# The delta rule's doubling levels with the upper chunk one bank behind the lower, and six remainders placed later in VectorE's order

## The chip, the cores and the metric

The program runs on one core of a Trainium2 chip. The metric is the device time of one execution in microseconds (us); before the change it is 2875.41 us, the median of three runs (2873.04 to 2876.01).

## The reference, cut to what matters

A 512-token sequence of width 1024 passes two layers of a first block and one layer of a second block. All matrices are float32. In each layer of the first block a quarter of the mixing width is a recurrent mixer of 4 heads of 64:

```python
def step(S, inp):
    r_t, w_t, k_t, v_t, kk_t, a_t = inp
    s_kk = jnp.einsum('bhvk,bhk->bhv', S, kk_t)
    S = (S * w_t[:, :, None, :] - s_kk[..., None] * (kk_t * a_t)[:, :, None, :]
         + v_t[..., None] * k_t[:, :, None, :])
    return S, jnp.einsum('bhvk,bhk->bhv', S, r_t)
...
mixed = jnp.concatenate([y_att, y_rwkv, y_conv], axis=-1) @ w_mix_out[l]
```

The second block has a gated delta rule of 8 heads, which the reference itself cuts into chunks of 64 tokens and solves with the inverse of a lower triangular matrix:

```python
a = jnp.einsum('bhnid,bhnjd->bhnij', k_beta, kc) * decay_strict
t_inv = lax.linalg.triangular_solve(eye + a, jnp.broadcast_to(eye, a.shape),
                                    left_side=True, lower=True, unit_diagonal=True)
...
def step(state, inp):
    q_e, at, u_c, w_c, k_d, dec = inp
    v_new = u_c - jnp.einsum('bhck,bhkv->bhcv', w_c, state)
    o = jnp.einsum('bhck,bhkv->bhcv', q_e, state) + jnp.einsum('bhij,bhjv->bhiv', at, v_new)
    state = state * dec[..., None, None] + jnp.einsum('bhck,bhcv->bhkv', k_d, v_new)
    return state, o
```

## The kernel before, in words

Most of the time is dense products of 128 by 128 weights with 512 tokens. The change touches only the recurrent mixers, which the kernel handles in chunks of 64 tokens, in both blocks by the same helpers, with a `Unit` object that names the tiles (`d_...` for the first block, once in each of its two layers; `gd_...` for the second block).

A group is 16 matrices of 64 by 64: four banks of PSUM (`level_bank(q)`, q = 0 to 3), in each two pairs j, and for each pair a lower chunk c = 0 on partitions 0 to 63 and an upper chunk c = 1 on partitions 64 to 127. The first block's mixer has 2 groups in each layer (4 chunks each), the second block's has 4 groups (2 chunks each): 8 groups in all. Each triangular inverse is built in five levels (LEVELS = 5, m = 0 to 4; 40 levels in all). A level is:

- `level_v_pe` on TensorE: for each bank q one product for each j and c (16 products). It waits for the masked factor `bt` from GpSimd (`delta_pool`) and, where m > 0, for the bank's subtraction of the level before (`delta_xy_ready`); in level 0 for `delta_start`, which VectorE gives for two banks at a time. After a bank it gives `delta_v1_summed`.
- `level_act` on ScalarE: copies the bank to `v1` and gives `delta_v1_ready`.
- `level_x_pe` on TensorE: for each bank the products for x (not in level 4) and y, for each j and c (32 products, 16 in level 4). After a bank it gives `delta_xy_summed`.
- `level_dve` on VectorE: subtracts the bank's sums from x and y (one instruction for each bank) and gives `delta_xy_ready`.

A product of chunk c reads 64 partitions and writes 64 partitions of the same half, so lower products lie in one 64 by 64 tile of TensorE's array and upper ones in the diagonally opposite tile. Each float32 product leaves two MATMUL records in the trace.

The inverse feeds a recursion over chunks: `read_pe` (L2143, L2151), `rhs_dve` (L2200, L2203), `solve_pe` (L2163, L2169), `u_act` (L2218), `update_pe` (L2179 to L2189), `state_dve` (L2210). The first group's levels run alone. In the first block (`rw_delta_pe`) the four chunks of the first group are then woven between the products of the second group's levels by a hand-written order; in that order a piece of the recursion stands between each x product and the next v product. In the second block (`gd_delta_pe`) the two chunks of group s are woven between the levels of group s + 1; there levels 0 and 1 follow each other directly. The last group's recursion runs alone. Every engine takes its instructions in the order in which they are written.

Six `others_low` instructions in each layer of the first block (L2295, on VectorE) form the low parts `hn_lo` of the six tiles of the mixed activations that the recurrent mixer doesn't make (four of attention, two of the convolution). TensorE wants them (`others_lo`) only after the whole recursion, for the output projection. Before the change four stand after levels 0 to 3 of the first group, and two among the second group's levels.

Of the kernel before, what the change touches and what calls it, by code (L numbers as in the profile page):

```python
# [12 lines left out]
P = 128  # L13
# [78 lines left out]
HD = 64  # L92
# [5 lines left out]
LEVELS = 5  # L98
# [23 lines left out]
OTHERS = (0, 1, 2, 3, 6, 7)  # L122


def program(nc, w, out):
# [23 lines left out]
    with ExitStack() as ctx:  # L149
# [262 lines left out]
        delta_bt_ready = sem("delta_bt_ready")  # L412
# [115 lines left out]
        def half(c):  # L528
            return slice(HD * c, HD * c + HD)

        def level_bank(q):
            return LEVEL_BANK + q
# [1510 lines left out]
        def level_v_pe(pe, d, s, m):  # L2043

            G = d.group + s
            i = LEVELS * G + m
            for q in range(4):
                pe.wait_ge(delta_bt_ready, 2 * i + q // 2 + 1)
                if m:
                    pe.wait_ge(delta_xy_ready, 4 * (i - 1) + q + 1)  # L2050
                else:
                    pe.wait_ge(delta_start, 2 * G + q // 2 + 1)
                for j in range(2):
                    for c in range(2):
                        last = pe.matmul(ps[half(c), level_bank(q), j * HD:(j + 1) * HD], d.bt[half(c), m % 2, q, j],  # L2055
                                         d.xy[half(c), q, j, 0], start=True, stop=True)
                last.then_inc(delta_v1_summed, 1)

        def level_x_pe(pe, d, s, m):

            i = LEVELS * (d.group + s) + m
            for q in range(4):
                pe.wait_ge(delta_v1_ready, 4 * i + q + 1)
                for j in range(2):
                    at = P + j * P
                    if m < LEVELS - 1:
                        for c in range(2):
                            pe.matmul(ps[half(c), level_bank(q), at:at + HD], d.xy[half(c), q, j, 1], d.v1[half(c), q, j],  # L2068
                                      start=True, stop=True)
                    for c in range(2):  # L2070
                        last = pe.matmul(ps[half(c), level_bank(q), at + HD:at + 2 * HD], d.v1[half(c), q, j], d.xy[half(c), q, j, 1],  # L2071
                                         start=True, stop=True)
                last.then_inc(delta_xy_summed, 1)

        def level_act(act, d, s, m):
            i = LEVELS * (d.group + s) + m
# [220 lines left out]
        def rw_delta_dve(dve, own, d, l):  # L2297
            rw_masks_dve(dve, d, 0)
            for m in range(LEVELS):
                if m == 0:  # L2300
                    rw_mc1_dve(dve, d, 0)
                level_dve(dve, d, 0, m)
                if m < LEVELS - 1:
                    others_low(dve, l, OTHERS[m])
            rhs_dve(dve, own, d, 0, 0)
            rw_masks_dve(dve, d, 1)
            state_dve(dve, d, 0, 0)
            rw_mc1_dve(dve, d, 1)
            rhs_dve(dve, own, d, 0, 1)
            level_dve(dve, d, 1, 0)  # L2310
            state_dve(dve, d, 0, 1)
            others_low(dve, l, OTHERS[4])
            level_dve(dve, d, 1, 1)
            rhs_dve(dve, own, d, 0, 2)
            others_low(dve, l, OTHERS[5])
            level_dve(dve, d, 1, 2)
            state_dve(dve, d, 0, 2)
            rhs_dve(dve, own, d, 0, 3)
            level_dve(dve, d, 1, 3)
            state_dve(dve, d, 0, 3)  # L2320
            level_dve(dve, d, 1, 4)
            for i in range(4):
                rhs_dve(dve, own, d, 1, i)
                state_dve(dve, d, 1, i)

        def spread_pe(pe, s):
# [597 lines left out]
```

## Time and profile before

| What | us |
|---|---|
| median of three runs | 2875.41 |
| the profiled execution | 2876.07 |
| its span in the profile | 2874.3 |
| TensorE busy | 2748.0 |
| VectorE busy | 1494.7 |
| ScalarE busy | 967.8 |
| GpSimd busy | 189.0 |

The three delta stages lie at 571 to 634 us, 1595 to 1659 us and 2561 to 2680 us of the span. Busy time is a union of the records of an engine. "PE" is TensorE's products, "PEld" its weight loads, "DVE" is VectorE, "ACT" ScalarE and "POOL" GpSimd. A stretch in which TensorE is busy need not be one in which it is at its peak: several tiles of its array can run at once, and a stretch in which only one runs counts the same.

### The profile page before, as it was taken

What the parts mean: (1) busy time and instruction counts of PE and PEld (TensorE: products, weight loads), DVE (VectorE), ACT (ScalarE), POOL (GpSimd) and SP (SyncE); (2) the same over time, 40 slices, a digit from 0 to 9 for tenths busy, and PEclk for the clock granted to TensorE, in tenths of its full rate; (3) what the DMA queues carried; (4) which work ended last, traced back from release to release, by engine and by line L of the source; (5) the groups of instructions that cost most, each with busy time, mean ns of one, the idle gap of its engine ahead of it and who ended that gap; (6) DMA issues with size and microseconds to landing.
All of it is one profiled execution on the core that took longest, in us unless ns stands there. A gap on an engine that the chain in (4) does not pass through costs nothing.

```text
span 2874.3 us, 42222 instructions
## 1 busy us (share of the span) xinstructions
PE 2748.0 (96%) x17756; PEld 2240.7 (78%) x17756; DVE 1494.7 (52%) x1845; ACT 967.8 (34%) x1471; POOL 189.0 (7%) x267
## 2 busy tenths in 40 slices
PE   6999999999999999999999899999999999968998
PEld 5888877687888878888777878888877777658787
DVE  6565565756565443333457644333365546755534
ACT  3222334523222332222345333222324444323322
POOL 3000000320000000000002300000010000013000
PEclk9999999989999999999999989999999999969999
DMA  7565542103566222232222012232232222100132
GB/s 287 200 218 203 191 167 72 52 18 112 202 207 220 88 85 102 86 112 88 95 80 71 3 59 90 88 108 93 90 103 74 66 74 69 61 1 3 56 103 73
DMA packets 46521, 299.68 MB, mean 104 GB/s; under 512 B 5664, under 2 KB 5792, under 8 KB 18080
## 3 DMA queue, kind: packets, MB, share of 16 engines
q1 hardware_dynamic: 37152, 230.35, 23.5%
q0 software_dynamic: 9216, 67.11, 6.5%
q8 instruction: 118, 1.93, 0.3%
q14 instruction: 35, 0.29, 0.0%
HBM read 295.35 MB, written 2.10 MB: 103 GB/s over the span
## 4 chain that ended last, share of the span: by engine, by line
PE 92%; DVE 5%; ACT 1%; DMA 1%; issue 1%; POOL 0%; SPq 0%; DVEq 0%; ACTq 0%
PE ps L921 18%; PE ps L922 18%; PE ps L923 18%; PE ps L1209 6%; PE ps L1210 6%; PE ps L1211 6%; PE ps L1516 2%; PE ps L1517 2%; PE ps L1518 2%; PE ps L2071 1%; PE ps L2055 1%; PE ps L2068 1%; DMA ada_first<-in_ada 1%; PE ps L1331 1%; PE ps L1295 1%
## 5 line engine op out<-in xcount | busy, mean ns | idle before, releaser
L921 PE MATMUL ps<-hn_hi,w_hi 128*128 128x512 f32 x1440 | 564.5, 392 | 16.9 <-DVE hn_lo L870 16.7
L922 PE MATMUL ps<-hn_lo,w_hi 128*128 128x512 f32 x1440 | 563.4, 391 | 0.0
L923 PE MATMUL ps<-hn_hi,w_lo 128*128 128x512 f32 x1440 | 562.9, 391 | 0.0
L897 DVE TENSOR_TENSOR w_lo<-w_raw,w_hi 128x2048 fp32r<-128x2048 f32 (+2 forms) x227 | 467.8, 2061 | 162.8 <-ACT w_hi L890 162.8
L890 ACT ACTIVATE w_hi<-w_raw 128x2048 fp32r<-128x2048 f32 (+2 forms) x227 | 390.6, 1721 | 100.0 <-PE ps L1211 97.3
L1209 PE MATMUL ps<-hn_hi,w_hi 128*128 128x512 f32 x776 | 323.6, 417 | 7.7 <-DVE hn_lo L870 4.9
L921 PEld LDWEIGHTS ps<-hn_hi,w_hi 128*128 128x128 f32 x1440 | 272.3, 189 | 75.3 <-issue 18.6
L923 PEld LDWEIGHTS ps<-hn_hi,w_lo 128*128 128x128 f32 x1440 | 272.3, 189 | 57.4
L922 PEld LDWEIGHTS ps<-hn_lo,w_hi 128*128 128x128 f32 x1440 | 272.4, 189 | 56.3
L1210 PE MATMUL ps<-hn_lo,w_hi 128*128 128x512 f32 x776 | 306.4, 395 | 0.0
L1211 PE MATMUL ps<-hn_hi,w_lo 128*128 128x512 f32 x776 | 305.8, 394 | 0.0
L921 PE MATMUL ps<-act_hi,w_hi 128*128 128x512 f32 x704 | 273.9, 389 | 0.0
L922 PE MATMUL ps<-act_lo,w_hi 128*128 128x512 f32 x704 | 273.9, 389 | 0.0
L923 PE MATMUL ps<-act_hi,w_lo 128*128 128x512 f32 x704 | 273.9, 389 | 0.0
L989 ACT ACTIVATE silu<-ps 128x512 f32<-128x512 f32 x88 | 52.7, 599 | 599.1 <-PE ps L923 599.1
L1035 DVE TENSOR_TENSOR act_f<-silu,ps 128x512 f32<-128x512 f32 x88 | 60.5, 687 | 370.5 <-ACT silu L989 370.5
L1209 PEld LDWEIGHTS ps<-hn_hi,w_hi 128*128 128x128 f32 x776 | 147.7, 190 | 54.4 <-issue 23.5
L1210 PEld LDWEIGHTS ps<-hn_lo,w_hi 128*128 128x128 f32 x776 | 148.3, 191 | 35.0 <-issue 6.2
L1211 PEld LDWEIGHTS ps<-hn_hi,w_lo 128*128 128x128 f32 x776 | 148.1, 191 | 32.5
L772 DVE CUSTOM_DVE_ANT_0 ada_w<-ada_w,c_row,b_ada 128x1024 f32<-128x1024 f32 x128 | 159.0, 1279 | 0.1
L1061 DVE SCALAR_TENSOR_TENSOR h<-act_f,out_gain,h 128x512 f32<-128x512 f32 (+1 forms) x64 | 48.1, 752 | 204.2 <-ACT act_f L1005 204.2
L923 PEld LDWEIGHTS ps<-act_hi,w_lo 128*128 128x128 f32 x704 | 132.1, 188 | 27.6
(470 smaller groups left out, 3630.9 us busy)
## 6 DMA issues: line engine op xcount, KB each, us to landing
w_raw<-in_up SPq DMA_DIRECT2D x88, 1024.0 KB, 4.9
ada_w<-in_ada POOLq DMA_DIRECT2D x64, 1024.0 KB, 5.2
w_raw<-in_down SPq DMA_DIRECT2D x64, 704.0 KB, 4.1
w_raw<-in_mix_in SPq DMA_DIRECT2D x20, 1024.0 KB, 4.9
w_raw<-in_dsa_in SPq DMA_DIRECT2D x18, 1024.0 KB, 4.9
w_raw<-in_merge SPq DMA_DIRECT2D x16, 768.0 KB, 4.3
ada_first<-in_ada SPq DMA_DIRECT2D x8, 1024.0 KB, 12.4
w_raw<-in_mix_out SPq DMA_DIRECT2D x8, 1024.0 KB, 4.9
```

The costliest lines, as they stand in the source:

```text
L772: last = dve.tensor_tensor_reduce(ws[:, t], ws[:, t], c_row[:], 1.0, b_ada[:, col:col + 1], ALU.mult, ALU.add, mod[:, col:col + 1])
L890: act.activation(w_hi[:, slot, 0:size], w_raw[:, slot, 0:size], ACT.Copy).then_inc(w_hi_ready, 1)
L897: dve.tensor_tensor(w_lo[:, slot, 0:size], w_raw[:, slot, 0:size], w_hi[:, slot, 0:size].bitcast(F32), ALU.subtract).then_inc(w_lo_ready, 1)
L921: pe.matmul(bank, wh, x_hi[:, k], start=(k == 0), stop=False)
L922: pe.matmul(bank, wh, x_lo[:, k], start=False, stop=False)
L923: return pe.matmul(bank, wl, x_hi[:, k], start=False, stop=(k == K - 1))
L1035: dve.tensor_tensor(act_f[:, s], silu[:, s], main[s][1], ALU.mult).then_inc(act_f_ready, 1)
L1209: pe.matmul(ps[:, t], wh, hn_hi[:, k], start=(k == 0), stop=False)
L1210: pe.matmul(ps[:, t], wh, hn_lo[:, k], start=False, stop=False)
L1211: last = pe.matmul(ps[:, t], wl, hn_hi[:, k], start=False, stop=(k == KD - 1))
L1516: pe.matmul(main[slot][t], wh, x_hi[:, kk], start=(kk == 0), stop=False)
L1517: pe.matmul(main[slot][t], wh, x_lo[:, kk], start=False, stop=False)
```

## The change

The products of a level keep their number, operands and results; their order and the places of the waits and signals change. Stage q of `level_v_pe` and of `level_x_pe` now holds the lower chunk's products of bank q beside the upper chunk's of bank q - 1, so there are five stages for four banks: in the first only lower products, in the last only upper ones. The wait for bank q stands ahead of the whole stage, and the signal for bank q - 1 after it. On VectorE the six `others_low` leave their places among the levels and stand in the last recursion of each layer, two each between `rhs_dve` and `state_dve` of the second group's chunks 0, 1 and 2 (`OTHERS` is (0, 1, 2, 3, 6, 7)).

```diff
+            def product(q, j, c):
+                return pe.matmul(ps[half(c), level_bank(q), j * HD:(j + 1) * HD], d.bt[half(c), m % 2, q, j],
+                                 d.xy[half(c), q, j, 0], start=True, stop=True)
+            for q in range(5):
+                if q < 4:
+                    pe.wait_ge(delta_bt_ready, 2 * i + q // 2 + 1)
+                    if m:
+                        pe.wait_ge(delta_xy_ready, 4 * (i - 1) + q + 1)
+                    else:
+                        pe.wait_ge(delta_start, 2 * G + q // 2 + 1)
                 for j in range(2):
-                    for c in range(2):
-                        last = pe.matmul(ps[half(c), level_bank(q), j * HD:(j + 1) * HD], d.bt[half(c), m % 2, q, j],
-                                         d.xy[half(c), q, j, 0], start=True, stop=True)
-                last.then_inc(delta_v1_summed, 1)
+                    if q < 4:
+                        product(q, j, 0)
+                    if q:
+                        last = product(q - 1, j, 1)
+                if q:
+                    last.then_inc(delta_v1_summed, 1)
...
+            for q in range(5):
+                if q < 4:
+                    pe.wait_ge(delta_v1_ready, 4 * i + q + 1)
                 for j in range(2):
                     if m < LEVELS - 1:
+                        if q < 4:
+                            x_product(q, j, 0)
+                        if q:
+                            x_product(q - 1, j, 1)
+                    if q < 4:
+                        y_product(q, j, 0)
+                    if q:
+                        last = y_product(q - 1, j, 1)
+                if q:
+                    last.then_inc(delta_xy_summed, 1)
...
                 level_dve(dve, d, 0, m)
-                if m < LEVELS - 1:
-                    others_low(dve, l, OTHERS[m])
...
             state_dve(dve, d, 0, 1)
-            others_low(dve, l, OTHERS[4])
             level_dve(dve, d, 1, 1)
             rhs_dve(dve, own, d, 0, 2)
-            others_low(dve, l, OTHERS[5])
...
             for i in range(4):
                 rhs_dve(dve, own, d, 1, i)
+                for j in OTHERS[2 * i:2 * i + 2]:
+                    others_low(dve, l, j)
                 state_dve(dve, d, 1, i)
```

## Rows read from the trace of the kernel before

**Rows 1.** The page: the chain that ended last, shares of the span by engine.

```profile
PE 92%; DVE 5%; ACT 1%; DMA 1%; issue 1%; POOL 0%; SPq 0%; DVEq 0%; ACTq 0%
```

**Rows 2.** Stretches: from:to, length, then busy us of each engine, granted clock.

```profile
core 0: us, PE busy (x) PEld busy (x) DVE busy (x) ACT busy (x) POOL busy (x), PEclk, DMA share, GB/s
594.00:620.00 26.00, 24.11 (x820) 23.74 (x812) 17.45 (x40) 7.81 (x27) 8.23 (x10) 1.00 0.02 4
...
2591.40:2594.80 3.40, 3.40 (x74) 3.40 (x70) 0.84 (x2) 0.55 (x2) 1.34 (x2) 0.50 0.02 5
...
625.40:639.00 13.60, 12.84 (x130) 9.66 (x125) 2.74 (x8) 4.81 (x7) 0.00 (x0) 0.50 0.00 1
```

**Rows 3.** TensorE in order of time, x products of level 2, both tiles at work.

```profile
586.92 0.31 PE L2068 MATMUL ps<-d_v,d_xy 64*64 64x64 f32 x4
587.04 0.31 PE L2071 MATMUL ps<-d_xy,d_v 64*64 64x64 f32 x4
587.16 0.31 PE L2068 MATMUL ps<-d_v,d_xy 64*64 64x64 f32 x4
```

**Rows 4.** TensorE around a solve, whose eight L2163 records share one tile.

```profile
616.50 0.45 PE L2163 MATMUL ps<-d_rhs,d_yf 64*64 64x64 f32 x5
616.74 0.27 PE L2169 MATMUL ps<-rw_vt,rw_kt 64*64 64x64 f32 x1
616.79 0.22 PE L2163 MATMUL ps<-d_rhs,d_yf 64*64 64x64 f32 x1
...
616.85 0.22 PE L2163 MATMUL ps<-d_rhs,d_yf 64*64 64x64 f32 x1
...
616.90 0.22 PE L2163 MATMUL ps<-d_rhs,d_yf 64*64 64x64 f32 x1
```

**Rows 5.** The same around a solve of the second block (16 records, one tile).

```profile
2604.80 0.27 PE L2055 MATMUL ps<-gd_xy,gd_bt 64*64 64x64 f32 x1
2604.85 0.22 PE L2163 MATMUL ps<-gd_rhs,gd_yf 64*64 64x64 f32 x1
...
2604.97 0.22 PE L2163 MATMUL ps<-gd_rhs,gd_yf 64*64 64x64 f32 x1
```

**Rows 6.** VectorE in order of time, levels 2 and 3 of a first group.

```profile
586.69 1.82 DVE L2089 TENSOR_TENSOR d_xy<-d_xy,ps 128x256 f32<-128x256 f32 x4 [0.50 <-PE ps L2071]
588.43 0.69 DVE L2295 TENSOR_TENSOR hn_lo<-proj,hn_hi 128x512 fp32r<-128x512 f32 x1
589.61 1.82 DVE L2089 TENSOR_TENSOR d_xy<-d_xy,ps 128x256 f32<-128x256 f32 x4 [0.50 <-PE ps L2071]
```

**Rows 7.** TensorE in order of time, the last bank's v products, the next x.

```profile
588.66 0.45 PE L2055 MATMUL ps<-d_xy,d_bt 64*64 64x64 f32 x8
588.91 0.22 PE L2068 MATMUL ps<-d_v,d_xy 64*64 64x64 f32 x1
```

**Rows 8.** TensorE's first v product of a group, and who TensorE waited for.

```profile
576.72 0.51 PE L2055 MATMUL ps<-d_xy,d_bt 64*64 64x64 f32 x10 [1.38 <-POOL d_bt L555]
...
PE ps L2055 <- DVE gd_xy L2369: 18.2, 8, 6.3
```

**Rows 9.** All six remainders of both layers: duration min/median/max in ns.

```profile
L2295 DVE TENSOR_TENSOR hn_lo<-proj,hn_hi x8: 683/684/686, 581.7 to 1615.3; 128x512 fp32r<-128x512 f32 x8
L2295 DVE TENSOR_TENSOR hn_lo<-conv_own,hn_hi x4: 1098/1106/1114, 605.8 to 1633.8; 128x512 fp32r<-128x512 f32 x4
```

**Rows 10.** VectorE in the last recursion of layer 0.

```profile
622.33 0.29 DVE L2210 TENSOR_TENSOR state<-state_p,ps 128x128 f32<-128x128 f32 x1 [1.56 <-PE ps L2179]
...
623.62 0.29 DVE L2203 TENSOR_TENSOR state_p<-state,chunk_decay 128x128 f32<-128x128 f32 x1
625.36 0.29 DVE L2210 TENSOR_TENSOR state<-state_p,ps 128x128 f32<-128x128 f32 x1 [1.44 <-PE ps L2179]
...
626.77 0.28 DVE L2203 TENSOR_TENSOR state_p<-state,chunk_decay 128x128 f32<-128x128 f32 x1
629.29 0.29 DVE L2210 TENSOR_TENSOR state<-state_p,ps 128x128 f32<-128x128 f32 x1 [2.24 <-PE ps L2179]
```

More of the change, by code:

```diff
@@ L2046, in level_v_pe @@
             i = LEVELS * G + m
[L2047 to L2052, printed above, removed]
-                for j in range(2):
-                    for c in range(2):
-                        last = pe.matmul(ps[half(c), level_bank(q), j * HD:(j + 1) * HD], d.bt[half(c), m % 2, q, j],
-                                         d.xy[half(c), q, j, 0], start=True, stop=True)
-                last.then_inc(delta_v1_summed, 1)
+            def product(q, j, c):
+                return pe.matmul(ps[half(c), level_bank(q), j * HD:(j + 1) * HD], d.bt[half(c), m % 2, q, j],
+                                 d.xy[half(c), q, j, 0], start=True, stop=True)
@@ L2059, in level_x_pe, with x_product, y_product @@
         def level_x_pe(pe, d, s, m):
             i = LEVELS * (d.group + s) + m
-            for q in range(4):
-                pe.wait_ge(delta_v1_ready, 4 * i + q + 1)
+            def x_product(q, j, c):
+                at = P + j * P
+                return pe.matmul(ps[half(c), level_bank(q), at:at + HD], d.xy[half(c), q, j, 1], d.v1[half(c), q, j],
+                                 start=True, stop=True)
+            def y_product(q, j, c):
+                at = P + j * P + HD
+                return pe.matmul(ps[half(c), level_bank(q), at:at + HD], d.v1[half(c), q, j], d.xy[half(c), q, j, 1],
+                                 start=True, stop=True)
@@ L2064, in level_x_pe @@
+            for q in range(5):
+                if q < 4:
+                    pe.wait_ge(delta_v1_ready, 4 * i + q + 1)
                 for j in range(2):
-                    at = P + j * P
                     if m < LEVELS - 1:
[L2067 to L2072, printed above, removed]
@@ L2073, in level_x_pe @@
-                last.then_inc(delta_xy_summed, 1)
+                        if q < 4:
[8 more added lines that the diff above has]
+                    last.then_inc(delta_xy_summed, 1)
         def level_act(act, d, s, m):
```

## Prediction

> **What bounds the kernel now.** I read the chain that ended last first: TensorE holds 92% of it [rows 1]. The change touches only the delta stages, some 240 us of the 2874, so I went on to the granted clock and busy time by stretch. In the stretch where the second group's levels are woven with the recursion, TensorE is busy 24.11 of 26 us at full clock [rows 2]; work added to its path there is added to the time. A busy TensorE isn't a full one, though, and this change is about which of its tiles runs when, so the rest rests on record starts.
>
> **Two tiles at once, before.** In x products eight records start in 587.16 - 586.92 = 0.24 us, 0.03 us each [rows 3]. A solve is a run of records that all lie in one tile: five records take 0.45 - 0.22 = 0.23 us from the first start to the fifth, 0.058 us each [rows 4]. So a tile takes one record each 0.058 us, and in the levels both chunks already run side by side at that rate, into the same bank. I call 0.058 us one slot. A level keeps each tile busy for 16 slots in v and 32 in x (16 in level 4); v and x make 48 slots, 2.80 us.
>
> **How far one tile runs ahead.** L2169 needs another tile than L2163's last records and starts at 616.74, when three L2163 records (616.79, 616.85, 616.90) haven't started; L2055 starts at 2604.80 when three records of a solve of the second block are due (2604.85, one left out, 2604.97) [rows 4, 5]. I read this as: instructions go out in order to a queue for each tile, which holds three records that haven't started, and a full queue holds back everything behind it. That is my choice between none and any distance; both ends are rivals below.
>
> **Loop of a first group, before.** Its levels 0 to 3 hand over with nothing between. From the fourth subtraction of one level to that of the next: 586.69 + 1.82 - 0.42 = 588.09 to 589.61 + 1.40 = 591.01, 2.92 us [rows 6]. The path: subtraction start to last bank's v products 588.66 - 588.09 = 0.57; these products to the x start 0.25; x start 588.91 to the next fourth subtraction 2.10 [rows 6, 7]. So a round trip sets 2.92, not the 2.80 of the tiles. The remainder after each level (588.43, 0.69 us) ends 0.50 us before VectorE's next work [rows 6].
>
> **Part 1, the lag, at a hand-over with nothing between.** The wait for bank 3 now holds back lower bank 3 and upper bank 2 (4 slots side by side), and upper bank 3 follows (4 more). The lower tile starts x after its 4. The upper x products stand behind ten lower records; the tenth goes out when the lower tile starts its seventh, so the upper x starts 6 slots after the lower one, at 4 + 6 = 10 slots instead of 4. A bank is signalled only after its upper half. Thus 6 slots, 6 x 0.058 = 0.35 us, are added to each round, 2.92 to 3.27. Such hand-overs: four in each of three first groups, and level 0 to 1 in the three later groups of the second block, 15. 15 x 0.35 = 5.2 us.
>
> **Part 1, with a piece of the recursion between.** The piece covers the later signal: the last upper record starts 6 slots later, and the next v reaches its third bank after 12 slots and the piece's 4 to 12. What stays is the upper tile's tail: eight upper records end x, the last goes out when the fourth from the end starts, so the lower tile idles 6 - 4 = 2 slots. With a piece that uses both tiles it can be 4. The four hand-overs of the second groups of two layers make 8, the other three of the second block's three later groups 9, together 17. At 2.5 slots, 0.15 us, nearer the 2 because most pieces use one tile first: 2.5 us. Ends: 0 (the second block's and the second groups' tiles are often skewed already, as in [rows 4]) and 4 slots, 4.0 us.
>
> **Part 1, ends of a group.** In level 0 the second bank's upper products come behind the wait for banks 2 and 3, which is long: 1.38 us in the first group, and 18.2 us in 8 waits in the second block [rows 8]. Then the upper tile has 12 slots of work where it had 8. 0 to 4 slots, of which the x lag hides some; I take 3, 0.17 us, for 8 groups 1.4 us. Level 4 has only y, 16 records: by the same count the lag is 2 slots, 0.12 us, 8 times 0.9 us. Queued behind the delayed signals are ScalarE's copies (idle most of the time), GpSimd's factors (made a level ahead) and VectorE's subtractions, then `rhs_dve` behind them in VectorE's order; for the last I count nothing extra since the piece comes later on TensorE too. At half clock slots double, which hits a level 0 x product in most groups (clock 0.50 at 2591.4 [rows 2]); this is inside the 4 slots above.
>
> **Part 2, the remainders.** What is taken from between the levels cost nothing (VectorE idles 0.50 us behind it) and gives nothing. In the last recursion VectorE issues them between L2203 and the update of the state, which waits for TensorE. Queued behind them is `state_dve`, and behind that TensorE's next read. Chunk 0: 1.56 us free, 2 x 0.69 = 1.38. Chunk 1: 623.62 + 0.29 + 1.38 = 625.29 against 625.36. Chunk 2: 626.77 + 0.28 + 2 x 1.106 = 629.26 against 629.29 [rows 9, 10]. All six fit, the last by 0.03 us and only because the clock is low from 625.4 [rows 2]. At full clock the wait would be chunk 1's 1.44, and 2.21 - 1.44 = 0.8 us would show, 1.6 in two layers. I take 0, range 0 to 1.6.
>
> **Sum.** 5.2 + 2.5 + 1.4 + 0.9 = 10.0 us on the profiled execution's 2876.07 (span 2874.3), 2886.1. The median lies 0.66 lower, so 2885.4 is forecast. Clock windows of 3.4 us at half rate lie at the groups' mask phases in the second block [rows 2]. Such a window costs at most 1.7 us of full-rate work, and the moved schedule may miss or gain one: 2 us either way. The forecast's own range is 2880.5 to 2892.
>
> **Rivals.**
>
> *Any distance ahead.* If tiles run freely past each other, the upper x starts right behind its own v products: the cost is the 4 slots that stand behind the bank 3 wait, 0.23 us at 15 hand-overs, 3.5 us, and nothing elsewhere. 2878.9. For it: the skew in [rows 4]. Against: in two places the other tile waits until just three are left, though it had been free. Chance 0.17.
>
> *In strict order.* If nothing passes a record of the other tile, each v runs its first and last stage in one tile (4 more slots), each x 8 more, level 4's 4: 32 x 12 + 8 x 8 = 448 slots, 26 us, 2901.4. Against: L2169 and L2055 start ahead of L2163 [rows 4, 5]. The Trainium skill, in "TensorE: Matmul & The Clock Gate", section "Part 3: Packing small matmuls", states this order ("strict FIFO, no reordering"); by that rule 2901.4 would come out. These rows disagree for starts across tiles. Chance 0.08.
>
> *Faster: the shared bank.* Before, both tiles write one bank at the same time; afterwards two. If the shared bank holds a tile up, it shows as slots longer than those of a lone tile. A solve's slot is 0.058 and a level's is 0.058, so the price is nought by the rows; the most that rounding leaves (0.001 us in a slot, 32 x 48 + 8 x 32 = 1792 slots) is 1.8 us. To be faster by 0.2% over the 10.0 us of the sum, a slot has to fall by 15.8 / 1792 = 0.009 us; that is the point from which this decides, and it gives 16.1 - 10.0 = 6.1 us, 2869.3. The skill's "TensorEngine Tiling (Array Packing)", section "Restrictions and Gotchas", says that different row tiles cannot access the same bank simultaneously. Had the hardware kept them apart, level records would start at a lone tile's spacing; the trace shows twice that rate. Chance 0.05.
>
> *The remainders don't fit.* With the high clock in chunk 2, 2887.0; it goes with the forecast.
>
> **How the numbers follow.** Forecast class 0.70 (of it 0.04 ends under 2881.2), any distance 0.17, strict order 0.08, faster 0.05. A measurement of this kernel tells about 0.2%, 5.8 us, from no change. Slower by more: 0.66 + 0.08 = 0.74. Within: 0.04 + 0.17 = 0.21. Faster: 0.05. The range for 8 in 10 takes in the freer rival and the upper bounds of the terms (5.2 + 4.0 + 1.9 + 0.9 + 1.6 and 2 for the clock, 2891), and goes some way to the strict order: 2877.5 to 2895.
>
> **What would show it.** First-group rounds of the fourth subtraction at 3.27 us instead of 2.92 (3.15 for any distance, 3.62 for strict order); at each x start a few records of the lower tile alone, spaced 0.058; the woven stretch longer by about 1 us; the wait before each state update in chunks 0 to 2 nearly gone but the state no later. It is wrong if the rounds stay at 2.92 or shorten, or if level records come closer than 0.03 us.

## The result, and the profile after

| | before | after |
|---|---|---|
| median of 4 and 4 runs, us | 2875.7 (2873.0 to 2881.0) | 2903.8 (2897.4 to 2906.4) |
| ratio, 95% interval | 1 | 1.0083 (1.0054 to 1.0112) |
| the same with 29 and 6 runs, later | 2876.7 (2872.1 to 2890.0) | 2901.4 (2888.5 to 2904.8), 1.0068 (1.0046 to 1.0090) |
| span of the profiled execution, us | 2874.3 | 2904.6 |

The change makes the kernel slower by 25 to 28 us. The forecast was 10 us, its upper end 2895. The sign is right, the size is not.

The chain of after has the same shares as in [rows 1], TensorE at 92%. The first new thing is the granted clock over the whole span, before and then after:

```profile
core 0: 2874.3 us, clock 0.972
```

```profile
core 0: 2904.6 us, clock 0.963
```

The second is where it fell. Stretches of before, first the woven part of layer 0 (from the first v copy of its second group to the first u copy of the last recursion), then a group of the last stage; columns as in [rows 2]:

```profile
599.50:621.30 21.80, 20.85 (x684) 20.58 (x681) 13.91 (x36) 7.41 (x26) 6.65 (x9) 1.00 0.02 4
...
2588.60:2616.40 27.80, 23.83 (x711) 23.09 (x707) 15.95 (x35) 8.94 (x33) 10.12 (x12) 0.94 0.02 4
```

And of after, the same two between the same marks, each followed by the part of it in which the clock was at half:

```profile
603.00:629.40 26.40, 24.64 (x683) 24.50 (x684) 12.81 (x36) 7.25 (x26) 6.66 (x9) 0.87 0.01 3
603.60:610.40 6.80, 6.08 (x110) 6.09 (x111) 2.53 (x7) 0.83 (x3) 3.40 (x5) 0.50 0.01 4
...
2609.70:2639.50 29.80, 26.33 (x704) 25.75 (x704) 15.79 (x36) 8.85 (x33) 10.20 (x13) 0.89 0.02 4
2610.70:2617.50 6.80, 5.67 (x102) 5.70 (x103) 2.00 (x4) 0.83 (x3) 3.02 (x4) 0.50 0.01 2
```

The woven part had full clock (1.00) before and has 6.8 us at 1.2 GHz now; it takes 26.4 us instead of 21.8. The group of the last stage has 6.8 us at that level where before had 3.4.

What TensorE did ahead of it is in its own order of time. The second group's first v products, in before (layer 1, its longer gap; in layer 0 it is 0.53 us) and in after (layer 0; in layer 1 it is 1.19 us): the products of banks 0 and 1, then the wait for the factors and masks of the other half:

```profile
1622.54 0.63 PE L2055 MATMUL ps<-d_xy,d_bt 64*64 64x64 f32 x15
1624.12 0.45 PE L2055 MATMUL ps<-d_xy,d_bt 64*64 64x64 f32 x8 [0.95 <-POOL d_bt L555]
```

```profile
602.26 0.67 PE L2049 MATMUL ps<-d_xy,d_bt 64*64 64x64 f32 x12
604.32 0.58 PE L2049 MATMUL ps<-d_xy,d_bt 64*64 64x64 f32 x6 [1.38 <-POOL d_bt L555]
```

The idle time grew from 0.53 and 0.95 us to 1.38 and 1.19: four upper records that used to run ahead of the wait now stand behind it. (The wait ends with GpSimd's factor at 604.26; VectorE's mask ends at 603.68.) Half rate begins at 603.6, in this gap. That the longer gap is why the clock falls looks plain here, and is not what the runs below show.

The rounds of a first group (the row of VectorE that answers to [rows 6]) go from 2.92 to 590.59 - 587.21 = 3.38 us, where 3.27 was predicted:

```profile
587.21 1.74 DVE L2109 TENSOR_TENSOR d_xy<-d_xy,ps 128x256 f32<-128x256 f32 x4 [2.57 <-PE ps L2077]
590.59 1.74 DVE L2109 TENSOR_TENSOR d_xy<-d_xy,ps 128x256 f32<-128x256 f32 x4 [1.64 <-PE ps L2077]
593.97 1.35 DVE L2109 TENSOR_TENSOR d_xy<-d_xy,ps 128x256 f32<-128x256 f32 x3 [1.64 <-PE ps L2077]
```

The remainders in the last recursion, chunks 1 and 2, answering to [rows 9, 10]:

```profile
631.97 1.29 DVE L2315 TENSOR_TENSOR hn_lo<-proj,hn_hi 128x512 fp32r<-128x512 f32 x2
633.30 0.29 DVE L2230 TENSOR_TENSOR state<-state_p,ps 128x128 f32<-128x128 f32 x1
...
634.79 1.29 DVE L2315 TENSOR_TENSOR hn_lo<-conv_own,hn_hi 128x512 fp32r<-128x512 f32 x2
636.93 0.29 DVE L2230 TENSOR_TENSOR state<-state_p,ps 128x128 f32<-128x128 f32 x1 [0.85 <-PE ps L2199]
```

They fit, with 0.16 us left in chunk 0, nothing in chunk 1 and 0.85 in chunk 2.

### The profile page after: what moved, and what is told of

Same layout as the page of the kernel before. It is cut to its first block, busy times and chain, and to the rows that moved or that the text cites. A ratio compares the mean times of both kernels' runs of the same rounds, so it can differ in the third digit from the quotient of the medians.

```text
span 2904.6 us, 42222 instructions
## 1 busy us (share of the span) xinstructions
PE 2780.3 (96%) x17756; PEld 2270.1 (78%) x17756; DVE 1492.1 (51%) x1845; ACT 968.0 (33%) x1471; POOL 187.3 (6%) x267
## 4 chain that ended last, share of the span: by engine, by line
PE 92%; DVE 5%; ACT 1%; DMA 1%; issue 1%; POOL 0%; SPq 0%; DVEq 0%; ACTq 0%
PE ps L921 18%; PE ps L923 17%; PE ps L922 17%; PE ps L1209 6%; PE ps L1211 6%; PE ps L1210 6%; PE ps L1516 2%; PE ps L1517 2%; PE ps L1518 2%; PE ps L2049 2%; PE ps L2077 1%; PE ps L2072 1%; DMA ada_first<-in_ada 1%; PE ps L1331 1%; PE ps L1295 1%
## 5 line engine op out<-in xcount | busy, mean ns | idle before, releaser
L921 PEld LDWEIGHTS ps<-act_hi,w_hi 128*128 128x128 f32 x704 | 132.2, 188 | 27.6
L922 PEld LDWEIGHTS ps<-act_lo,w_hi 128*128 128x128 f32 x704 | 132.2, 188 | 27.4
```

What stands on the lines that cost most here:

```text
L921: pe.matmul(bank, wh, x_hi[:, k], start=(k == 0), stop=False)
L922: pe.matmul(bank, wh, x_lo[:, k], start=False, stop=False)
```

## Experiments

Theory A: the lag alone costs, by the slots of the two tiles (a slot is the 0.058 us that one tile needs for a record). B: the remainders cost. C: a good part is the clock. Ratios are to runs of before on the same chip (its medians: 2878.9 for the first four kernels, 2880.6 for the next eight, 2876.7 for the last four).

### Which edit, and which half of it

**lag_only**: of the change's hunks the first alone, both level functions.

> Both level helpers as changed, the remainders left where they were. Theory A (the lag alone costs): the whole excess of the change, 20 us or more over before, with rounds of the fourth subtraction in a first group at 3.38 us. Theory B (the moved remainders cost a share): at least 3 us less than the whole change. Theory C (about a third of the excess is the clock, which happens to fall in this run's windows and not in the kernel's): a mean near +13 us with a wide spread, and about as many half-rate microseconds as before (165).

**rem_only**: the reverse, that is

```diff
                 level_dve(dve, d, 0, m)
-                if m < LEVELS - 1:
-                    others_low(dve, l, OTHERS[m])
...
-            others_low(dve, l, OTHERS[4])
...
-            others_low(dve, l, OTHERS[5])
...
                 rhs_dve(dve, own, d, 1, i)
+                for j in OTHERS[2 * i:2 * i + 2]:
+                    others_low(dve, l, j)
                 state_dve(dve, d, 1, i)
```

> Only the six remainders moved, the levels as before. Theory A: within 1 us of before, the three state updates of chunks 0 to 2 no later than before. Theory B: 1.6 us slower or more. A gain from VectorE freed between the levels would show as first-group rounds under 2.92 us; I expect 2.92.

**v_lag**: of the change, `level_v_pe` alone.

> Only the v products lag. By counting slots with a queue of three per tile: at a hand-over with nothing between, bank 3's upper products come 4 slots later, and x starts beside them with nothing waiting: 4 slots, 0.23 us on 2.92 = 3.15 us; with the first record after a wait counted 0.3 us. 15 x 0.23 + level 0 and pieces 2 us = +5 to +6 us. If the clock carries a large share and falls because level 0's products are spread over two waits, v alone gives more than half of the whole excess, +12 us or more.

**x_lag**: `level_x_pe` alone.

> Only the x products lag. By counting slots: the upper x products start 6 to 7 slots after the lower ones and nothing else moves: 0.35 to 0.41 us on 2.92 = 3.27 to 3.33 us a round, 15 x 0.38 + 17 x 0.15 + 1 = +9 us. v_lag and x_lag together then exceed the pair (their lags overlap). If strict order ruled, x alone would give 3.38 and +19 us.

| | median us | ratio, interval | first-group round | clock, profiled |
|---|---|---|---|---|
| lag_only | 2902.8 | 1.0074 (1.0057 to 1.0091) | 3.38 | 0.965 |
| rem_only | 2877.1 | 0.9991 (0.9976 to 1.0005) | 2.92 | 0.972 |
| v_lag | 2890.8 | 1.0035 (1.0024 to 1.0045) | 3.15 | 0.965 |
| x_lag | 2901.7 | 1.0073 (1.0058 to 1.0088) | 3.28 | 0.964 |

The rounds of v_lag (3.15 us) and of x_lag (3.28), each from its own VectorE:

```profile
586.50 1.82 DVE L2096 TENSOR_TENSOR d_xy<-d_xy,ps 128x256 f32<-128x256 f32 x4 [1.66 <-PE ps L2078]
...
589.65 1.82 DVE L2096 TENSOR_TENSOR d_xy<-d_xy,ps 128x256 f32<-128x256 f32 x4 [0.73 <-PE ps L2078]
```

```profile
586.22 1.74 DVE L2102 TENSOR_TENSOR d_xy<-d_xy,ps 128x256 f32<-128x256 f32 x4 [1.88 <-PE ps L2070]
...
589.50 1.74 DVE L2102 TENSOR_TENSOR d_xy<-d_xy,ps 128x256 f32<-128x256 f32 x4 [0.94 <-PE ps L2070]
```

B falls: the remainders make no difference that shows. A is right about the place: the whole loss comes with the level functions. C in the form recorded for lag_only (a mean near +13 us, as much half rate as before) did not come either, +24 us did. But x_lag, expected at +9 us, loses 23 with a round of 3.28 us, near the 3.27 that the slots give: most of its loss is not in its rounds. And the halves don't add up, neither in time (12 + 23 us against 24) nor in the round (0.23 + 0.36 us against 0.46); v_lag too loses 12 where slots gave 5 to 6. What all three share is a clock of 0.964 or 0.965.

### How far one tile runs ahead

**x_runs**: nothing lags; within a bank the lower products come first, then the upper ones.

```diff
                 pe.wait_ge(delta_v1_ready, 4 * i + q + 1)
-                for j in range(2):
-                    at = P + j * P
-                    if m < LEVELS - 1:
-                        for c in range(2):
...
+                for c in range(2):
+                    for j in range(2):
+                        at = P + j * P
+                        if m < LEVELS - 1:
...
```

> The kernel before, but in each bank of the x and y products the eight lower records come first and the eight upper ones behind them, in the same bank, behind the same wait; nothing lags by a bank. It tests the queue that the prediction assumed (three records of a tile may wait ahead of the issue, so that the other tile's records still start beside them). By it the upper tile starts a bank one to three slots later than now and each bank ends at most that much later, because the two tiles no longer end together: between 1 and 4 slots of 0.058 us a round, rounds of 2.98 to 3.15 us where before has 2.92, and 2 to 7 us in all. By strict order, in which a tile stands idle while the other's records pass, every bank takes twice its 8 slots: a round of 4 us or more, and over 30 us in all. By free order at any distance: rounds of 2.92 us and no change. The half-rate time should stay near the 157 us of before (the sum of the stages), unless the levels become slower by more than 0.2 us a round.

Measured: 2904.6 us, 1.0076 (1.0046 to 1.0106). The four banks of a round in x_runs:

```profile
589.83 0.42 DVE L2088 TENSOR_TENSOR d_xy<-d_xy,ps 128x256 f32<-128x256 f32 x1 [0.75 <-PE ps L2070]
590.41 0.42 DVE L2088 TENSOR_TENSOR d_xy<-d_xy,ps 128x256 f32<-128x256 f32 x1 [0.15 <-PE ps L2070]
590.98 0.42 DVE L2088 TENSOR_TENSOR d_xy<-d_xy,ps 128x256 f32<-128x256 f32 x1 [0.15 <-PE ps L2070]
591.56 0.42 DVE L2088 TENSOR_TENSOR d_xy<-d_xy,ps 128x256 f32<-128x256 f32 x1 [0.15 <-PE ps L2070]
...
593.33 0.42 DVE L2088 TENSOR_TENSOR d_xy<-d_xy,ps 128x256 f32<-128x256 f32 x1 [0.75 <-PE ps L2070]
```

A bank takes 0.575 us, ten slots, and the round 3.50, where I expected 3.15 at most. Recounted after the result: in a queue of three the last of eight records goes out when the fifth starts, four slots after the first; if the other tile then starts a slot later, two such hand-overs a bank make ten slots. That extra slot is read from these rows. Without it a queue of three would give eight, and a queue of two ten, so the number three is good to about a slot. In strict order it would be 16 slots, 0.93 us; with any distance 8, 0.47 us as before. Both rivals on the order fall.

### Is the clock lower because everything comes later?

The stretch from the preparation of the last stage to its first group holds no changed instruction, yet took 124.3 us in before and 129.1 in after. **shift_a** and **shift_b** are before with a first product of an input piece repeated 44 and 40 times some 700 us ahead of it, **after_shift** is after with 4 repeats:

```diff
+                for _ in range(again if t == k == 0 else 0):
+                    pe.matmul(ps[:, t], wh, hn_hi[:, k], start=True, stop=True)
                 pe.matmul(ps[:, t], wh, hn_hi[:, k], start=(k == 0), stop=False)
```

> The kernel before with its levels untouched; 44 more matmuls of 512 columns (a first product of an input piece repeated, each overwriting the same sums) stand early in the second part, behind both recurrent layers and some 700 us ahead of the last delta stage, so that all that follows comes about 9.4 us later with TensorE busy all the while. It asks whether the stretch from the preparation of the last delta stage to its first group (124.3 us in before, 129.0 in every kernel with a lag, at 41 and 55 us of half rate, with no instruction of it changed) is longer because of where a mere delay puts it. If a delay is enough, this kernel shows 129 us there and ends 9.4 + 4.7 = 14 us later, about 2893; if it isn't, it shows 124.3 us and ends 9.4 us later, about 2888. The groups of the last stage should stay at 24.3, 27.8, 26.8 and 23.1 us if their clock follows from their own idle time, and move by some 1.5 us each if it follows from the delay.

> shift_a with 40 repeated matmuls instead of 44: everything behind them comes 0.9 us earlier than in shift_a and some 8.9 us later than in before, again with TensorE busy all the while and no level changed. In shift_a the stretch from the preparation of the last stage to its first group took 124.34 us at 41.0 us of half rate, as in before. If that stretch's clock hangs on exactly where it lies, a delay that differs by 0.9 us can change it: then it takes about 129 us at 55 us of half rate here, as in every kernel with a lag, and this kernel, with less work than shift_a, is some 4 us slower than it, about 2890 against 2886.9. If the lagged kernels had the 129 us for another reason, this stretch stays at 124.3 us and the kernel is 0.9 us faster than shift_a.

> The kernel after with 4 repeated matmuls of 512 columns at the same place, a delay of 0.9 us ahead of the last stage. The other side of shift_b: if the place decides, the stretch may fall back from 129.1 to 124.3 us, and with it the half-rate stretch of 6.8 us at 2494.6 us that before hasn't; the kernel with more work is then 3 to 4 us faster than after, about 2899. If the lag decides, it is 0.9 us slower, about 2904, and the stretch stays at 129 us.

Measured 2886.9 (1.0021; 1.0006 to 1.0037), 2884.8 (1.0024; 1.0006 to 1.0041) and 2899.7 (1.0067; 1.0049 to 1.0086). The stretch in shift_a, shift_b, after_shift, then in fill4_before (below), whose code up to there is that of before, and in after:

```profile
2450.20:2574.50 124.30, 98.30 (x464) 64.83 (x464) 78.05 (x69) 42.50 (x47) 3.41 (x4) 0.83 0.11 36
```

```profile
2448.20:2574.10 125.90, 99.94 (x464) 66.06 (x464) 78.07 (x69) 42.62 (x46) 3.38 (x4) 0.82 0.11 36
```

```profile
2443.00:2570.80 127.80, 102.97 (x462) 68.76 (x460) 78.56 (x69) 42.66 (x47) 3.84 (x4) 0.80 0.11 35
```

```profile
2439.20:2567.90 128.70, 103.97 (x463) 69.05 (x463) 78.05 (x68) 42.60 (x46) 3.36 (x4) 0.79 0.11 35
```

```profile
2455.20:2584.30 129.10, 104.34 (x463) 69.09 (x461) 78.56 (x69) 42.78 (x46) 3.68 (x4) 0.78 0.11 35
```

Neither clean outcome came. The repeats in shift_a delay what follows by 10.0 us in this profile and leave the stretch as it was; those in shift_b delay it by 8.9 and it is 1.6 us longer. But fill4_before shows nearly the whole 129 us with nothing changed ahead of it: the same instructions run at a mean clock of 0.79 in one execution and 0.83 in another. So the 4.8 us are no fixed price of the lag. Of the ten profiles with a lag or with x_runs' order none is under 127.8 us, of the eight others two are above 127; whether the change makes the longer form likelier is open.

The delay does reach the last stage. shift_a's levels are those of before, yet in two of its three later groups the half rate lasts 6.8 us, as in after, and not 3.4; shift_b has the same. The first of them in shift_a:

```profile
2598.20:2605.00 6.80, 4.69 (x90) 4.72 (x91) 2.91 (x6) 0.84 (x4) 3.95 (x5) 0.50 0.02 5
```

So the 6.8 us in after's last stage are no sign of the lag by themselves. The recurrent woven parts are: shift_a and shift_b have no half rate there.

### Is the clock lower because of the gaps?

**fill_after**, **fill_before**: in units behind the first, matmuls nobody reads, into columns not in use at that time, ahead of the first v products (last stage) and between their second and third bank. This does add work, it leaves none out.

```diff
+        def fill_pe(pe, d, s, n):
+            if d.more:
+                for _ in range(n):
+                    pe.matmul(ps[:, S2, P:2 * P], d.key_q[:, 0, 0:P], d.key_q[:, 0, 0:P], start=True, stop=True)
+            else:
+                pe.wait_ge(gd_e_logs, s + 1)
+                for _ in range(n):
+                    pe.matmul(ps[:, E_BANK], d.key_q[:, 0, 0:P], d.key_q[:, 0], start=True, stop=True)
...
+                if s and m == 0 and q == 2:
+                    fill_pe(pe, d, s, 20 if d.more else 8)
...
+                fill_pe(pe, d, s + 1, 5)
                 level_v_pe(pe, d, s + 1, 0)
```

> The kernel after, and in the units behind the first TensorE is given matmuls that nobody reads, in the time in which it waits for the masks: 20 of 128 columns between the second and the third bank of a recurrent unit's first v products (a gap of 1.60 us in after, 0.75 and 1.17 us in before, behind which after's new half-rate stretches at 603.6 and 1634.5 us begin), and in the last stage 5 of 512 columns ahead of a unit's first v products and 8 ahead of its third bank (gaps of 1.45 and 2.4 us). If the clock falls because of these gaps, the new stretches of 6.8 us in the woven parts are gone and those of 6.8 us in the last stage shrink, the woven part takes 23.5 to 24.5 us instead of 26.4, each group of the last stage some 1.5 to 2.5 us less than 29.8, 30.2 and 26.1 us, and the kernel comes at about 2892. If the clock falls for another reason (the sparser matmuls of the lagged levels themselves), the half-rate time stays near 206 us and the time within 3 us of 2902, or longer if the added matmuls delay the first products.

> The kernel before with the same added matmuls, but 8 of 128 columns in the recurrent units, whose gap is shorter here. In the last stage each group has a gap of 1.45 and one of 2.3 us ahead of a half-rate stretch of 3.4 us. If the gaps bring the clock down, these three or four stretches are gone and each gives back at most half its length: 1 to 1.7 us, 3 to 6 us in all, about 2873 to 2876 where before stands at 2878.9. If they don't, the half-rate time stays at 157 us and the time is that of before or a few us more. It is also the version that would beat both kernels if the theory of the gaps holds.

Measured 2919.7 us, 1.0136 (1.0109 to 1.0163), and 2902.1, 1.0079 (1.0050 to 1.0108). The clock did what the theory of the gaps says: in the woven parts and in the last stage's later groups no half rate is left in either. The fillers were far too long (a matmul here leaves two records; one of 512 columns takes 1.06 us, not 0.53), so the time says nothing. **fill2_** cuts them to 128 columns, 8 and 14 of them (10 in after's recurrent units, none in before's), still sized as if a matmul left one record:

> fill_before with the added matmuls cut to the gaps: one of 128 columns took 0.12 us there and one of 512 columns 0.53 us, so the 5 and 8 of 512 filled 2.65 and 4.25 us where the gaps are 1.45 and 2.3 us, and held back the first products by some 3.1 us a group. Here 8 of 128 columns (1.0 us) stand in the first gap, 14 (1.7 us) in the second, and none in the recurrent units, which have no half-rate stretch in before. If the clock stays up as it did in fill_before, a group of the last stage loses nothing to the fillers and gains what the half rate cost: 26.5 us instead of 27.8, 26.8 for the first two, 1 to 1.5 us each, 3 to 4 us in all, about 2877 where before stands at 2880. If 30.2 us (fill_before's 33.3 less the 3.1) is what a group takes at full rate, the clock costs nothing there, and the kernel is at or above before.

> The kernel after with the same cut fillers in the last stage, and 10 of 128 columns (1.2 us) in the gap of 1.60 us of the recurrent units. If the clock falls because of the gaps, the half-rate stretches at 603.6 and 1634.5 us and those of the last stage's groups are gone as in fill_after, now without the cost of the fillers: the woven parts take 24.0 to 24.7 us instead of 26.4, the groups of the last stage 28 to 28.5 instead of 29.8, 30.2 and 25 instead of 26.1, and the kernel comes some 7 us below after, about 2896. Against fill2_before, both without these half-rate stretches, it shows what the lag itself costs in a group: 1.55 to 2.0 us by fill_after against fill_before.

Measured 2876.5, 0.9981 (0.9970 to 0.9992), and 2892.3, 1.0041 (1.0026 to 1.0056). **fill3_** has 5 and 9 (5 in after's recurrent units), **fill4_before** 3 and 6; **after_again** is after itself beside them. From fill2_after to fill3_after:

```diff
-                    fill_pe(pe, d, s, 10 if d.more else 14)
+                    fill_pe(pe, d, s, 5 if d.more else 9)
...
-                fill_pe(pe, d, s + 1, 8)
+                fill_pe(pe, d, s + 1, 5)
```

> fill2_before with 5 and 9 added matmuls instead of 8 and 14. One of them leaves two records of 0.12 us each, so it takes 0.24 us; the 8 and 14 took 1.9 and 3.4 us in gaps of 1.45 and 2.3 us, TensorE was busy 27.05 of 27.10 us of such a group, and the groups were some 1.5 us longer than they had to be. The 5 and 9 take 1.2 and 2.1 us. If the clock stays up, the groups take 25.6 us instead of 27.1 (27.8 and 26.8 in before), the last one 21.5 instead of 22.7, and the kernel comes 4 us below fill2_before: 2872 to 2873 where before stands at about 2879. If this much is too little to hold the clock, the groups show 3.4 us of half rate again and stay at 27 us.

> The same with 3 and 6 added matmuls, 0.7 and 1.4 us, half of the gaps. It tells whether half the gap is enough: the groups at 25.6 us and no half rate (2872) if it is; 3.4 us of half rate in each and the time of before (2879) if a gap that is half full brings the clock down as an empty one does.

> The kernel after with 5 added matmuls (1.2 us) in the recurrent gap of 1.6 us and 5 and 9 in the last stage's. fill2_after's 10 took 2.4 us in that gap of 1.6 and held the third bank back. With the clock up, the woven parts take 23.8 us instead of 24.7 (26.4 in after) and the groups of the last stage 27.5 and 23.0 instead of 29.0 and 24.2. Against fill3_before, equally free of added stalls, the difference is the price of the lag without its clock: 13 to 16 us, so about 2887.

> The kernel after as it is, beside the fillers and the kernel before on the same chip, for the size of its own loss in more runs: the four so far gave 1.0083, and lag_only, which differs by the remainders alone, 1.0074 in six. If the remainders are free, as in rem_only, it comes at 1.0074 to 1.0083 times before, 2900 to 2904. The part that the fillers bring back (fill3_after against it) is then what the gaps cost through the clock: some 13 us.

| | median us | ratio, interval |
|---|---|---|
| fill3_before | 2877.9 | 0.9995 (0.9983 to 1.0007) |
| fill4_before | 2876.3 | 0.9998 (0.9986 to 1.0011) |
| fill3_after | 2889.8 | 1.0036 (1.0023 to 1.0050) |
| after_again | 2901.4 | 1.0068 (1.0046 to 1.0090) |

The woven part of layer 0 and the first later group of the last stage in fill3_after, then the same in fill3_before:

```profile
600.00:623.70 23.70, 23.17 (x693) 22.84 (x694) 12.68 (x36) 7.16 (x26) 6.68 (x9) 1.00 0.01 4
...
2593.00:2620.20 27.20, 27.15 (x733) 26.41 (x734) 15.67 (x35) 8.70 (x32) 10.02 (x13) 1.00 0.02 4
```

```profile
600.20:622.00 21.80, 20.72 (x685) 20.45 (x681) 14.06 (x36) 7.40 (x26) 6.79 (x9) 1.00 0.02 4
...
2590.10:2616.60 26.50, 25.95 (x738) 24.93 (x733) 15.74 (x35) 8.85 (x33) 9.96 (x12) 1.00 0.02 4
```

With five added matmuls in a gap of 1.4 us the woven part's clock is 1.00 instead of 0.87 and its 26.4 us are 23.7. None of the six woven parts in fill_after, fill2_after and fill3_after has half rate; of the fourteen in the seven profiles with a lag or with x_runs' order and no filler, thirteen have. A filled gap keeps the clock up. But the length of the gap is not what tells the kernels apart. The idle time ahead of the third bank, and the woven part, layer 0 and layer 1 of one profile each:

| | order of the levels | gap, us | woven part, us | its clock |
|---|---|---|---|---|
| before | as before | 0.53, 0.95 | 21.8, 22.9 | 1.00, 1.00 |
| shift_b | as before | 1.33, 1.23 | 22.5, 23.2 | 1.00, 1.00 |
| x_lag | v as before, x lagged | 1.14, 1.12 | 24.7, 24.7 | 0.93, 0.93 |
| v_lag | v lagged, x as before | 1.38, 1.38 | 24.6, 24.7 | 0.93, 0.93 |
| after | both lagged | 1.38, 1.19 | 26.4, 26.3 | 0.87, 0.87 |
| after_shift | both lagged | 1.38, 1.38 | 25.2, 23.7 | 0.93, 1.00 |
| fill3_after | both lagged | filled | 23.7, 23.7 | 1.00, 1.00 |

The rows of shift_b in layer 0, of x_lag in layer 0 and of after_shift in layer 1:

```profile
600.00 0.51 PE L2058 MATMUL ps<-d_xy,d_bt 64*64 64x64 f32 x10 [1.33 <-POOL d_bt L555]
```

```profile
602.97 0.44 PE L2055 MATMUL ps<-d_xy,d_bt 64*64 64x64 f32 x7 [1.14 <-POOL d_bt L555]
```

```profile
1628.81 0.74 PE L2052 MATMUL ps<-d_xy,d_bt 64*64 64x64 f32 x17 [1.38 <-POOL d_bt L555]
```

A gap of 1.33 us between levels in the old order costs no clock, and one of 1.14 with a lag in x alone does. So in the woven parts the clock fell where a gap and a changed order stood together, and with either taken away it did not. Even together they don't settle it: after_shift's code is that of after until both recurrent layers are done, and its layer 1 ran at full clock behind a gap of 1.38 us, in 23.7 us with no filler:

```profile
1627.50:1651.20 23.70, 21.95 (x684) 21.81 (x684) 12.69 (x36) 7.14 (x26) 6.67 (x9) 1.00 0.01 3
```

The fillers give after 2901.4 - 2889.8 = 11.6 us back, from 6 and 12 executions that overlap (2888 to 2905 and 2882 to 2896), so it is good to some 6 us. Not all of it is shown to lie in the filled parts: in the last recursion of each layer, which holds no filler, fill3_after takes some 2 us less than after, and so does after_shift, which has none anywhere. For before they give nothing that lasts: fill2_before's 0.9981 was not met by its two shorter successors, so no version here clearly beats before. A group of the last stage does gain from the clock: the first in fill3_before takes 26.5 us against 27.8, and in fill4_before, whose gaps are half filled, the three take 26.9, 25.7 and 21.5 us without half rate, against 27.8, 26.8 and 23.1. The whole kernel stays the same in both, where 2872 was expected; in fill4_before's profile the stretch ahead of the groups takes 4.4 us more than in before.

The pairs with fillers give the lag's own price with the clock up in both: 2892.3 - 2876.5 = 15.8 us (fill2, over-long fillers) and 2889.8 - 2877.9 = 11.9 us (fill3). The runs say the same by their clocks. Beside fill3, executions of before span 2870 to 2874 us at 0.972 and 2886 and 2888 at 0.965; after_again spans 2886.7 at 0.972 and 2898.6 at 0.965: 13 to 16 and 10 to 12 us apart at an equal clock. The profiles of before and after_shift, both at 0.972, are 2874.3 and 2887.1 us, of which 0.9 are after_shift's repeats: 12 us. Each price from the medians is uncertain by some 5 us.

### What a lag costs with a piece between

The pair fill2 has rounds of the second kind at full clock. VectorE in the last stage's third group, in fill2_before (3.79 and 3.94 us) and fill2_after (4.16 and 4.32):

```profile
2630.08 1.82 DVE L2101 TENSOR_TENSOR gd_xy<-gd_xy,ps 128x256 f32<-128x256 f32 x4 [2.33 <-PE ps L2083]
...
2633.87 1.75 DVE L2101 TENSOR_TENSOR gd_xy<-gd_xy,ps 128x256 f32<-128x256 f32 x4 [0.79 <-PE ps L2083]
2637.81 1.82 DVE L2101 TENSOR_TENSOR gd_xy<-gd_xy,ps 128x256 f32<-128x256 f32 x4 [2.19 <-PE ps L2083]
```

```profile
2641.33 1.74 DVE L2121 TENSOR_TENSOR gd_xy<-gd_xy,ps 128x256 f32<-128x256 f32 x4 [3.03 <-PE ps L2089]
...
2645.49 1.67 DVE L2121 TENSOR_TENSOR gd_xy<-gd_xy,ps 128x256 f32<-128x256 f32 x4 [1.22 <-PE ps L2089]
2649.81 1.74 DVE L2121 TENSOR_TENSOR gd_xy<-gd_xy,ps 128x256 f32<-128x256 f32 x4 [2.65 <-PE ps L2089]
```

Each is 0.37 or 0.38 us longer. TensorE shows why. In fill2_before x starts at 2629.35 with both tiles and the piece behind it (`read_pe`, L2155) 1.69 us later:

```profile
2629.35 0.33 PE L2080 MATMUL ps<-gd_v,gd_xy 64*64 64x64 f32 x4
...
2631.04 0.27 PE L2155 MATMUL ps<-state,gd_kbg 64*64 64x64 f32 x1
```

In fill2_after the lower tile starts alone; two records start together first at 2640.54, 0.40 us or seven slots later, and the piece (L2175) starts at 2642.23, 2.09 us behind the start of x:

```profile
2640.14 0.33 PE L2084 MATMUL ps<-gd_v,gd_xy 64*64 64x64 f32 x2
2640.30 0.28 PE L2089 MATMUL ps<-gd_xy,gd_v 64*64 64x64 f32 x2
2640.42 0.28 PE L2084 MATMUL ps<-gd_v,gd_xy 64*64 64x64 f32 x2
2640.54 0.22 PE L2089 MATMUL ps<-gd_xy,gd_v 64*64 64x64 f32 x1
2640.54 0.27 PE L2084 MATMUL ps<-gd_v,gd_xy 64*64 64x64 f32 x1
...
2642.23 0.27 PE L2175 MATMUL ps<-state,gd_kbg 64*64 64x64 f32 x1
```

## Why the prediction was right and wrong

**The slot and the queue of three**: right in kind. Records of one tile pass those of the other up to a short distance, neither none nor any; ten slots a bank in x_runs fit neither rival on the order. The hand-over to the other tile comes about a slot later than I counted. Strict order's 2901.4 us is within 3 us of the result by chance: its rounds would be 3.62 us and were 3.38, and x_runs would have shown 16 slots. A time that fits doesn't make the mechanism; the rounds told them apart. The Trainium skill, "TensorE: Matmul & The Clock Gate", section "Part 3: Packing small matmuls", gives strict order ("strict FIFO, no reordering"); by that rule a bank of x_runs would take 0.93 us, and these rows (0.575) don't agree for records of different tiles.

**The shared bank**: it costs nothing that shows. In after the two tiles write different banks, and the records still come 0.06 us apart in each (two from 2640.30, the next at 2640.42). The Trainium skill's "TensorEngine Tiling (Array Packing)", section "Restrictions and Gotchas", says that different row tiles cannot access the same bank simultaneously; in before these two do write the same bank at 0.03 us a record over both [rows 3], so for this pair of tiles the rows don't agree.

**Hand-over with nothing between**: mechanism right, size low. Six slots (0.35 us) were predicted; the upper x products start seven slots behind the lower ones and the round grows by 3.38 - 2.92 = 0.46 us, eight slots. Over 15 hand-overs 6.9 us instead of 5.2.

**With a piece of the recursion between**: this step failed, by some 4 us. I asked how long the lower tile idles (2 slots) and took the rest as covered. What counts is when the piece is issued: it stands in order behind the last upper record, so it starts seven slots later, and everything behind it too. 0.37 or 0.38 us instead of 0.15, 17 times, is 6.4 us instead of 2.5; it is measured in the last stage at full clock and carried over to the other hand-overs.

**Ends of a group**: 2.3 us were taken. A later group of the last stage grew by 1.95 us at full clock (27.0 to 27.1 us in fill2_before, 29.0 in fill2_after); its four hand-overs account for about 0.46 + 3 x 0.37 = 1.57, which leaves 0.38 where 0.17 + 0.12 was counted. The pair fill3 doesn't repeat this: the same groups grow by 0.7 and 0.6 us there (26.5 and 27.3 to 27.2 and 27.9), since fill3_before's own rounds in them are longer (the first ones 4.67 and 4.46 us, against 4.15 in fill2_before). This term stays uncertain. The sum with the measured rounds, 6.9 + 6.4 + 2.3 = 15.6 us, lies at the upper one of the two prices (11.9 and 15.8).

**The remainders**: right, nothing, but not for the reason given. They were said to fit in chunk 2 only because the clock is low there, with 2.21 us for the two of them. They take 1.29. In after_shift the clock was full in this recursion, the case that was to cost 0.8 us, and they fit with 0.16 us to spare:

```profile
632.60 1.29 DVE L2318 TENSOR_TENSOR hn_lo<-conv_own,hn_hi 128x512 fp32r<-128x512 f32 x2
634.05 0.29 DVE L2233 TENSOR_TENSOR state<-state_p,ps 128x128 f32<-128x128 f32 x1 [0.16 <-PE ps L2202]
```

**The clock**: this step failed most. It was priced at 2 us either way, from the stretches that before has. With the lag, gaps in level 0 that the old order passes at full clock are followed by half rate: the woven parts, which had none in before, got 6.8 us of it each in after. In the last stage's later groups 6.8 us stand where before had 3.4, and there a mere delay does as much. Filling the gaps gives 11.6 us back, within some 6. I had written that half clock "is inside the 4 slots", which priced the slots at half clock and not the slots that newly fall under it. In all, 12 to 16 us for the lag and some 12 for the clock make the 25 to 28. Not settled are two things: what about the lagged order makes the clock fall behind a gap, and the part outside the delta stages, which varies between executions of the same code.

## What to carry to other kernels

In an in-order queue with a short look-ahead, price a reordering by when the *next* instruction can be issued, not by how long a unit idles; cover that stands behind the delayed records in the same queue is no cover. When a change thins out TensorE's work around a wait, the clock can fall on what follows: read the gaps and the granted clock of each stretch together, and test by filling the gap before explaining the time by the order. Then test the other half too: look for a kernel in which the same gap did no harm, since a remedy that works does not show that the gap's length was the cause. Count what one instruction leaves in the trace before sizing anything by its records.

## What the runs showed of the hardware

- A gap of TensorE of 1.38 us among lagged levels was followed by 6.8 us at 1.2 GHz (clock 0.50 from 603.6 us in after), and in one of two places in after_shift by none. Gaps of 0.53 to 1.33 us among levels in the old order were not (14 woven parts in seven profiles), nor was a gap with five matmuls in it that nobody reads (1.2 us).
- The same instructions over 124 us ran at a mean clock of 0.83 or 0.79 in different executions, and 29 executions of before alone span 2870 to 2888 us, the longest two at 0.965, the shortest two at 0.972 and 0.973.
- A record of one 64x64 tile can start ahead of about three earlier records of the diagonally opposite tile [rows 4, 5]. Eight records of one tile written ahead of eight of the other take 0.575 us a bank in x_runs; alternating they take 0.47, and one after the other they would take 0.93.
- The subtractions of 128x512 that took 1098 to 1114 ns (conv_own) between the levels [rows 9] take 683 to 692 in the last recursion. The tile is not the reason: in lag_only, where they stand between the levels as in before, one takes 1175 ns and the other 693. In before, each starts while a masking instruction of GpSimd is running (605.78 after 605.60). The fast one in lag_only starts first (615.41), and GpSimd's instruction, started at 615.48, takes 1.21 us instead of 0.73. So the one that starts second is the longer one in these rows; which part of the chip they share was not tested.
